# Block two's expert results are added to the tokens' sums one by one instead of through a sorted buffer

## What is computed

```python
hdn = silu(xc @ w1[e]) * (xc @ w3[e])            # 256 wide
ffn = sum over the token's two experts of weight * (hdn @ w2[e])
x = layernorm(DEEPNORM_ALPHA * x + g2 * ffn, ln2_g, ln2_b)
```

## Time and profile before

| | |
|---|---|
| Time, median of 3 runs | 989.95 us (989.67 to 990.65) |
| The profiled execution's own time | 991.67 us |
| Its span | 989.1 us |
| PE busy | 913.5 us (92%) |
| DVE busy | 547.4 us (55%) |
| ACT busy | 346.2 us (35%) |
| Read from HBM | 287.34 MB |
| Mean granted TensorE clock | 0.982 of full speed |

### The profile page before, as it was taken

The page is one execution under the profiler, slowest core; times in us unless marked ns, Lnnn a source line. Parts: engine busy times, 40 slices in busy tenths (PEclk is TensorE's granted clock), DMA queues, the critical chain, the costliest instruction groups (busy, mean ns, idle before and its releaser), DMA issues. The chain is left out here.

```text
span 989.1 us, 14610 instructions
## 1 busy us (share of the span) xinstructions
PE 913.5 (92%) x5308; PEld 552.8 (56%) x5308; DVE 547.4 (55%) x1106; ACT 346.2 (35%) x663; POOL 21.0 (2%) x41
## 2 busy tenths in 40 slices
PE   8999999999999998877787799999899999999995
PEld 6778656977967633322222389867643434343434
DVE  5736427555445747433333475887856655555556
ACT  5644434446345232221221356743531111111113
POOL 1000110000000000000000000000000000000000
PEclk9999999999999999998999899999999999999998
DMA  9355394455415999999999957530749999999931
GB/s 356 139 209 201 117 433 174 146 208 187 173 74 192 383 420 428 425 424 426 428 424 428 426 176 316 212 128 12 287 151 409 424 427 427 425 429 426 422 152 42
DMA packets 28894, 289.04 MB, mean 292 GB/s; under 512 B 3080, under 2 KB 5544, under 8 KB 7728
## 3 DMA queue, kind: packets, MB, share of 16 engines
q1 hardware_dynamic: 25344, 282.04, 69.0%
q0 software_dynamic: 1136, 3.74, 1.2%
q10 hardware_dynamic: 2368, 2.64, 0.9%
HBM read 287.34 MB, written 1.06 MB: 292 GB/s over the span
## 5 line engine op out<-in xcount | busy, mean ns | idle before, releaser
L1070 PE MATMUL bank<-ring,arena 128*64 128x512 f32 (+1 forms) x1024 | 188.9, 634 | 35.4 <-DMA ring<-in_experts 34.6
L508 DVE TENSOR_TENSOR ring_r<-ring,ring_r 128x1024 fp32r<-128x1024 f32 (+1 forms) x84 | 99.2, 1211 | 83.3 <-ACT ring_r L501 83.3
L1070 PEld LDWEIGHTS bank<-ring,arena 128*64 128x64 f32 (+1 forms) x1024 | 49.7, 126 | 131.0 <-issue 109.6
L501 ACT ACTIVATE ring_r<-ring 128x1024 fp32r<-128x1024 f32 (+1 forms) x84 | 84.8, 1046 | 74.4 <-PE bank L677 72.9
L675 PE MATMUL bank<-HT_r,ring_r 128*128 128x256 f32 x352 | 101.9, 289 | 2.6 <-DVE ring_r L508 1.8
L677 PE MATMUL bank<-HT_r,ring_r 128*128 128x256 f32 x352 | 99.6, 283 | 0.0
L1085 PE MATMUL bank<-ring,arena 128*64 128x512 f32 (+1 forms) x512 | 97.5, 609 | 0.3 <-DVE arena L2454 0.2
L1733 ACT ACTIVATE arena<-bank 128x512 f32<-128x512 f32 x64 | 38.2, 597 | 128.9 <-PE bank L1070 128.9
L676 PE MATMUL bank<-XN_r,ring_r 128*128 128x256 f32 x288 | 81.5, 283 | 0.0
L1727 ACT ACTIVATE arena<-arena 128x64 f32<-128x64 f32 (+1 forms) x64 | 18.1, 283 | 174.7 <-DVE arena L2444 174.7
L2419 DVE SCALAR_TENSOR_TENSOR arena_r<-bank,arena,arena_r 128x512 fp32r<-128x512 f32 x32 | 24.0, 750 | 97.6 <-ACT arena_r L1739 97.6
(11 more groups left out here) (472 smaller groups left out, 1457.1 us busy)
## 6 DMA issues: line engine op xcount, KB each, us to landing
ring<-in_experts SPq DMA_DIRECT2D x63, 2048.0 KB, 16.2
ring<-in_experts SPq DMA_DIRECT2D x63, 1024.0 KB, 13.5
ring<-in_ada SPq DMA_DIRECT2D x12, 2048.0 KB, 10.9
ring<-in_win SPq DMA_DIRECT2D x5, 2048.0 KB, 12.3
ring<-in_hy SPq DMA_DIRECT2D x3, 2048.0 KB, 19.8
ring<-in_mk SPq DMA_DIRECT2D x2, 2048.0 KB, 11.2
ring<-in_mv SPq DMA_DIRECT2D x2, 2048.0 KB, 12.0
ring<-in_wo SPq DMA_DIRECT2D x2, 2048.0 KB, 7.4
```

Source lines behind the costliest of these rows:

```text
L501: nc.scalar.activation(R(h), w, ACT.Copy).then_inc(sem("w_high"), 1)
L508: nc.vector.tensor_tensor(R(w), w, R(h), ALU.subtract).then_inc(sem("w_low"), 1)
L1070: last = mm(gu_bank[g:g + wide, :], xw[:, k, :], w[:, k * 512:(k + 1) * 512], start=k < sides, stop=k >= KD - sides)
```

## The change

Block two's experts work as block one's do. The four sums live in banks 0 to 3 from the router on: `start_sum` comes in two pairs, ahead of the gate's row and behind the counts, in place of some of the matmuls without a use. The gather has only banks 4 to 7, each used twice. VectorE makes the lists in place of `selw`. In a step, `down` adds both halves of the hidden part in one bank (128 rows: 64 slots for each half of the channels), VectorE multiplies by weight and gate in one instruction to `y_gated`, ScalarE rounds that to `y_high`, VectorE subtracts to `y_low`, and `to_tokens` takes the place of `down_T`. The gate's row is kept as `g2half`, 512 columns with another half of the channels in each half of the rows. The last expert's `down` moves behind the extras; `swT`, `ysT`, `pairs_T` and `scatter` are gone, and the three matmuls without a use inside an extra pass too.

```diff
-EXPERT = (4, 5, 6, 7)
-SUMS = (1, 2, 3, 4)
+EXPERT = {1: (6, 7, 5, 0), 2: (4, 5, 6, 7)}
...
-        + [(f"cnt{b}", 1)] + [("g2r", 2, (0, 1))] * (b == 2) + [(f"gx{b}", 8, ((3, 4, 5, 6, 7, 0, 1, 2), (4, 5, 6, 7, 0, 1, 2, 3))[b - 1])] \
-        + ([("bias", 1, (5,)), ("slots1", 1, (0,)), ("sct1", 4, SUMS)] if one else
-           [("swT2", 2, (6, 7)), ("yTa2", 4, EXPERT), ("sct2", 4, (0, 1, 2, 3)), ("yTb2", 4, EXPERT)])
+        + ([("cnt1", 1)] if one else [("sct2", 4, (0, 1, 2, 3)), ("cnt2", 1, (6,)), ("g2r", 2, (7, 4))]) \
+        + [(f"gx{b}", 8, ((3, 4, 5, 6, 7, 0, 1, 2), (4, 5, 6, 7, 4, 5, 6, 7))[b - 1])] \
+        + ([("bias", 1, (5,)), ("slots1", 1, (0,)), ("sct1", 4, (1, 2, 3, 4))] if one else [("slots2", 1, (5,))])
...
-                occupy(f"cnt{b}", 0, 6 if b == 2 else 8)
                 if b == 2:
-                    gate_row("g2r", diag2, "diag2")
+                    pe.wait_ge(sem("diag2"), 1)
+                    start_sum((0, 1))
+                    occupy("cnt2", 0, 2)
+                    pe.wait_ge(sem("diag2"), 2)
+                    gate_row("g2r", diag2)
...
-                occupy(f"gx{b}", 0, 6)
+                if b == 2:
+                    start_sum((2, 3))
+                occupy(f"gx{b}", 0, 6 if b == 1 else 1)
...
+                pe.wait_ge(sem("lists"), b)
+                ps = take(pe, f"slots{b}")
+                full(slot_lists(b, ps), f"slots{b}")
...
+                    ready(pe, "gx2", 4)
+                    for _ in range(3):
+                        mm(bank[EXPERT[2][0]][:, 0:256], ident, T("iota")[:, 0:256], start=True, stop=True)
...
                 def down(w, hb=hb):
-                    for half in range(2):
-                        for f in range(2):
+                    for f in range(2):
+                        for half in range(2):
                             o = f * D + half * 512
-                            g = wide * (f if b == 2 else 2 * half + f)
-                            last = mm(d_bank[half if b == 2 else 0][g:g + wide, :], hb[:, f, :], w[:, o:o + 512],
-                                      start=True, stop=True)
+                            g = 64 * half + 32 * f * (b == 1)
+                            last = mm(d_bank[g:g + wide, :], hb[:, f, :], w[:, o:o + 512],
+                                      start=b == 1 or f == 0, stop=b == 1 or f == 1)
...
-                    if 0 not in first and b == 1:
-                        pe.wait_ge(sem("y_low1"), e - 1)
-                        to_tokens(r % 2).then_inc(sem("to_tokens1"), 1)
-                    elif 0 not in first:
-                        pe.wait_ge(sem(f"d_lo{b}"), e - 1)
-                        pe.wait_ge(sem(f"d_hi{b}"), e - 1)
-                        if 2 not in first:
-                            pe.wait_ge(sem(f"y_out{b}"), e - 2)
-                        down_T().then_inc(sem(f"yT_done{b}"), 1)
+                    if 0 not in first:
+                        pe.wait_ge(sem(f"y_low{b}"), e - 1)
+                        to_tokens(r % 2).then_inc(sem(f"to_tokens{b}"), 1)
...
                 def weigh(e, i):
-                    act.wait_ge(sem("cur1"), e + 1)
-                    act.wait_ge(sem("down_done1"), e + 1)
-                    A_(R(y_high), d_bank[0][:, :], ACT.Copy, scale=cur[:, i, 1:2]).then_inc(sem("y_high1"), 1)
+                    if b == 1:
+                        act.wait_ge(sem("cur1"), e + 1)
+                        act.wait_ge(sem("down_done1"), e + 1)
+                    else:
+                        act.wait_ge(sem("y_gated2"), e + 1)
+                    high_part(i).then_inc(sem(f"y_high{b}"), 1)
...
+                def gated(i):
+                    return V.scalar_tensor_tensor(out=y_gated, in0=d_bank[:, :], scalar=cur[:, i, 1:2], in1=g2half,
+                                                  op0=ALU.mult, op1=ALU.mult)
...
                 def low_part(e, i):
+                    if b == 2:
+                        dve.wait_ge(sem("down_done2"), e + 1)
+                        gated(i).then_inc(sem("y_gated2"), 1)
+                    dve.wait_ge(sem(f"y_high{b}"), e + 1)
+                    y_rest(i).then_inc(sem(f"y_low{b}"), 1)
```

The extra pass of block two is now block one's. On VectorE it begins with three numbers read from the table and six instructions, and TensorE's `gate_up` waits for the last of them:

```diff
+                        s = dve.value_load(tabi[0:1, bass.ds(XSTART + j, 1)], min_val=0, max_val=NPAIR)
+                        rank = dve.value_load(tabi[0:1, bass.ds(XRANK + j, 1)], min_val=0, max_val=S - wide)
+                        ex = dve.value_load(tabi[0:1, bass.ds(XEXPERT + j, 1)], min_val=0, max_val=NE - 1)
+                        V.tensor_copy(xwin[:, 0], xsT[:, :, bass.ds(s, wide)])
+                        V.tensor_copy(turn_x[:, 0:wide], iota[:, bass.ds(rank, wide)]).then_inc(sem(f"cur{b}"), 1)
+                        dve.wait_ge(sem(f"cur{b}"), j * 3 + (NE + 1))
+                        rank_of_slot(b, turn_x[:, 0:wide]).then_inc(sem(f"extra_x{b}"), 1)
```

More of the change, by code:

```diff
@@ L445, in expert_banks @@
         def expert_banks(b):
-            if b == 1:
-                return bank[6], bank[7], [bank[5], bank[0]], None
-            base = place("yTa2", 0)[0]
-            at = [bank[(base + i) % 8] for i in range(6)]
-            return at[4], at[5], at[0:2], at[2:4]
+            return [bank[i] for i in EXPERT[b]]
         def slot(i):
@@ L1144, in step @@
                     if 1 not in first:
+                        if isinstance(e, int) and e == 1:
+                            ready(pe, f"slots{b}")
                         pe.wait_ge(sem(f"gu_sb{b}"), e)
@@ L1216, in moe @@
-                pe.wait_ge(sem("d_lo2"), NE)
-                pe.wait_ge(sem("y_out2"), NE - 1)
-                down_T(range(4))
-                pe.wait_ge(sem("d_hi2"), NE)
-                down_T(range(4, KD)).then_inc(sem("yT_done2"), 1)
+                pe.wait_ge(sem(f"y_low{b}"), NE - 1)
+                to_tokens(0).then_inc(sem(f"to_tokens{b}"), 1)
+                pe.wait_ge(sem("routed"), b)
+                n = pe.value_load(tabi[0:1, XCOUNT:XCOUNT + 1], min_val=0, max_val=NX[b] - 1)
@@ L1223, in moe @@
                         w = ring[:, slot(base), :]
-                        pe.wait_ge(sem("extra_x2"), j + 1)
-                        pe.wait_ge(sem("extra_w2"), j * 16 + 16)
-                        gate_up(xwin[:, 0], w).then_inc(sem("extra_gu2"), 1)
-                        pe.wait_ge(sem("extra_gs2"), j + 1)
-                        gu_T().then_inc(sem("extra_gT2"), 1)
-                        for _ in range(3):
-                            mm(d_bank[0][:, 0:256], ident, T("iota")[:, 0:256], start=True, stop=True)
@@ L1242, in pairs_T @@
-                def pairs_T(stage, js):
-                    for j in js:
-                        pt, half = j // 2, j % 2
-                        ps = take(pe, stage, j % 4)
-                        for c in range(4):
-                            last = tr(ps[:, c * P:(c + 1) * P], ysT[:, 4 * half + c, pt * P:(pt + 1) * P], ident)
-                        full(last, stage, j % 4)
-                def scatter(pt):
-                    stage = (f"yTa{b}", f"yTb{b}")[pt // 2]
-                    end = pt == NPAIR // P - 1
-                    for q in range(4):
-                        t, half = (q // 2, q % 2) if end else (q % 2, q // 2)
-                        ready(pe, stage, 2 * (pt % 2) + half)
-                        tok, cols = slice(t * P, (t + 1) * P), slice(half * 512, (half + 1) * 512)
-                        mm(acc[2 * t + half][:, :], R(swT[:, pt, tok]), R(ytok[:, pt, cols]), start=False, stop=False)
-                        last = mm(acc[2 * t + half][:, :], R(swT[:, pt, tok]), R(ytok_low[:, pt, cols]),
-                                  start=False, stop=end)
-                        if end:
-                            full(last, f"sct{b}", 2 * t + half)
@@ L1265, in moe @@
-                pairs_T(f"yTa{b}", range(0, 4))
-                scatter(0)
-                pairs_T(f"yTb{b}", range(4, 6))
-                scatter(1)
-                pairs_T(f"yTb{b}", range(6, 8))
-                scatter(2)
-                scatter(3)
+                        pe.wait_ge(sem(f"extra_x{b}"), j + 1)
+                        pe.wait_ge(sem(f"extra_w{b}"), j * 16 + 16)
+                        gate_up(xwin[:, 0], w).then_inc(sem(f"extra_gu{b}"), 1)
+                        slot_lists(b, list_bank)
@@ L1273, in _ @@
+                pe.wait_ge(sem(f"y_low{b}"), NE)
+                to_tokens(1, True)
             moe(1)
@@ L1697, in moe @@
                 if b == 2:
-                    copies("g2r", [g2row[:, 0:512], g2row[:, 512:1024]])
+                    for j in range(2):
+                        ps = got(act, "g2r", j)
+                        rows = slice(64 * j, 64 * j + 64)
+                        free(A_(g2half[rows, :], ps[rows, :], ACT.Copy), "g2r", j)
                 for k in range(0, KD, 2):
@@ L2609, in moe @@
[L2609 to L2619 removed]
+                            dve.wait_ge(sem("extra_down2"), j + 2)
```

364 lines of the change are left out of this document (101 added, 263 removed).

## The result

| | before | with the change |
|---|---|---|
| Time, median | 989.95 us (988.92 to 991.73, 9 runs) | 993.47 us (991.48 to 995.17, 9 runs) |
| The profiled execution's own time | 991.67 us | 991.48 us |
| Its span | 989.1 us | 988.9 us |
| PE busy | 913.5 us | 901.3 us |
| DVE busy | 547.4 us | 517.6 us |

The ratio after to before is 1.0027, 95% interval 1.0016 to 1.0038: 2.7 us slower (1.6 to 3.7); the two medians of the table lie 3.5 us apart. The forecast was 991.3 us, within a range of 987.6 to 995.2. The measured median lies 2.2 us above the forecast and inside the range. Measured a second time beside other runs of the kernel before, the ratio was 1.0015 (1.0004 to 1.0026). The prediction counts less than 0.2% as no change: the first measurement lies just beyond that, the second within it.

The account below looks back on a forecast made before the run. TensorE was taken as the bound (busy 92%, alone in the chain of block two's experts). Router +0.6, step +2.6, end -4.7 and clock +3.0 make +1.5 us: about 991.3 us, rounded down from the 989.95 median; range 987.6 to 995.2.

Parts of the forecast that it names:

- the router's term: Block two's router: VectorE starts earlier but the four-bank gather stalls, first `gate_up` 0.6 us later; bounds 0 and +1.5.
- the step: Block two's expert loop: `to_tokens` for `down_T` lengthens each of 29 steps by 0.09 us, +2.6 us; bounds 0 and +6.
- the end: Last `gate_up` to the last layer norm's first read: 31.9 us instead of 36.6, so -4.7 us.
- the clock: Tail: TensorE's waits bring two low stretches (half clock, 1.2 GHz), +3.0 us; bounds 0 and +10.
- within 0.2%: Whole kernel: time changes by less than 0.2% (2 us), counted as no change; chance 0.44.
- slower: Whole kernel: slower by more than 0.2%; chance 0.36.
- the forecast's own 989.5 to 993: Whole kernel: the time range of the forecast itself, without the rivals; chance 0.45.
- the rival with three or four low stretches: Tail: clock stays low for three or four stretches, +3.6 to +5.3 us, 993.5 to 995.3 us; chance 0.18.
- the first rival: Tail: the clock holds or falls once, sum -1.5 to 0, 988.4 to 990 us; chance 0.22.
- The rival of adds side by side: Loop: adds run in pairs, step shrinks by 0.24 us until weights bound it, -6.5 us, 983.5 us; chance 0.10.
- The slack of the weights: Last expert: gate and up weights land 5.4 us before TensorE wants them, so shorter steps gain at most that.

Follow-up runs that it names:

- Experiment 2: Kernel before, with one of `down_T`'s eight transposes done twice in every step: 995.19 us, ratio 1.0032.
- experiment 1: Changed kernel, with matmuls without a use ahead of each of TensorE's five waits in block two's tail: 990.55 us, ratio 0.9990.
- experiment 3: Changed kernel, with block two's `to_tokens` adding only the high part except for the last expert: 989.40 us, ratio 0.9978.
- e9: Changed kernel, with the three dropped matmuls without a use put back in block two's extra pass: 993.85 us, ratio 1.0029.
- experiment 6: Changed kernel, last expert's `down` ahead of the extra pass, window copied earlier, separate buffers; three runs: 983.71, 984.20 (with matmuls without a use), 982.52 us (repeat).
- experiment 4: Changed kernel, its extra pass copying the window and releasing `gate_up` before the two other table reads and the ranks: 992.85 us, ratio 1.0009.
- e7: Changed kernel, last expert's `down` ahead of the extra pass, window copied earlier, plus matmuls without a use in TensorE's waits: 984.20 us, ratio 0.9926.
- e6: Changed kernel, last expert's `down` ahead of the extra pass, window copied earlier, no matmuls without a use: 983.71 us, ratio 0.9919.

## Why the prediction came out as it did

The forecast had four terms, three of them with the right sign, and its sum, +1.5 us, was lower than the +2.7 of the first measurement and equal to the second's. Part of that is luck: by the profiles the router's term was 0.8 us too high, and the step, the end and the clock 0.6, 0.5 and 0.7 too low. The forecast gave "within 0.2%" a chance of 0.44 and "slower" 0.36, so what the first measurement shows was not its likeliest outcome. The median of 993.47 us also lies above the forecast's own 989.5 to 993, next to the rival with three or four low stretches; the traces show two. Step by step:

- **The step: right, a size off.** +0.09 us was predicted from block one's rows, and 0.11 was measured, so +2.6 became +3.2. `to_tokens` takes 0.12 us more than `down_T` up to `down`'s start, and `down` keeps the 1.87 us that it takes behind `down_T`. For that case the prediction's upper bound had 0.2 us a step, which was too much. There is no idle time ahead of `to_tokens` or `down`. Experiment 2 makes the same loss by another means and finds it whole at the end.
- **The router: wrong sign, small.** +0.6 was predicted and -0.2 measured. The gather stalled for 0.51 us and not 1.4. (By its own numbers the prediction's stall was 1.3: 720.6 and 0.74 make 721.3.) The step that failed is the start of VectorE's reading: I kept the 0.67 us of idle time ahead of it that the trace of before shows, behind two table reads. In the changed kernel these reads happen earlier, the first at 715.9 us, while VectorE still works off instructions that it already has, and the reading starts at 717.60 with no idle time. Before, both stood behind a wait of VectorE (at 720.9 and 721.5). That the missing wait is the cause is read from these times; no run tested it.
- **The end: right within 0.5 us once the clock is taken out.** 31.9 us was predicted without the clock, and experiment 1 shows 32.4. (Two sums in that count are 0.1 us off, 25.3 and not 25.4 behind the first hops, which moves nothing.) The extra pass's `gate_up` starts 14.7 us behind the last one and not 13.85: the reads and the branch leave VectorE idle for 2.09 us, where I took 1.2 (the bounds 0.7 and 2.5 held it). All later distances were met within 0.2 us: `gate_up` to `down` 7.12 (predicted 7.1), to `to_tokens` 4.18 (4.35), to the last `down` 1.12 (1.1), to the layer norm 5.31 (5.45). Against the 36.7 us of before the end gives -4.2, where -4.7 was predicted.
- **The clock: right, and somewhat larger.** Two low stretches were predicted for +3.0 (1.7 and 1.3), and two were found: on the extra pass's `gate_up`, as named, +1.94, and on a later group, the last `down`, +1.52. Two further groups lost 0.1 and 0.3 us. Together it is +3.7, as the tails of the changed kernel and of experiment 1 tell (36.1 and 32.4). This term decides the result: with the clock held the change comes out at 0.9990, which can't be told from no change, as the first rival said. By the Trainium skill ("TensorE: Matmul & The Clock Gate", section "Part 1: The HAM clock gate (the "warmup" mystery)") the low level is the default and activity lifts it; the tails agree with that, 0.99 with the waits filled (experiment 1) and 0.81 with waits of 1.65 to 4.60 us. All four profiles with a wait of 4.5 to 5.1 us ahead of the extra pass's `gate_up` (the change and its repeat, experiment 3 and e9) have it slow, 5.41 to 6.28 us.
- **The rival of adds side by side: the mechanism is there, the gain isn't.** A matmul of the gather, 512 columns with 128 rows, takes 0.235 us (7.52 by 32); the eight adds with 64 rows take 1.14 to `down`'s start, 0.142 each, and in experiment 3 four of them take 0.67, so that the other four cost 0.47, 0.118 each, half a gather's. I read this as adds that run in pairs already, and did in block one's rows that I had priced them by; no run put the halves in another order to test it. By the Trainium skill ("TensorE: Matmul & The Clock Gate", section "Part 3: Packing small matmuls — row/col tiling") matmuls in different row groups run at the same time, and the estimate of 0.86 us that I made from it (0.85 by its own terms) comes near the 0.94 (8 by 0.118) that the adds cost at the margin; the rest of the 1.14, 0.20, is what such a group costs beyond them. The rival's error was to count as a further gain what the row already contained.
- **The slack of the weights: wrong.** I gave it as 5.4 us, by adding the median landing time (15.7 us) to the last request. But the landing times grow along the loop; for the requests between 760 and 775 us the median is 13.1. This is the view of DMA issues in the trace of before again, for the request of 920.75 alone:

```profile
ring<-in_experts SPq DMA_DIRECT2D x1, 2048.0 KB, 20.0
```

It landed at 940.75, 1.0 us ahead of the `gate_up` that wants it (941.76). Experiment 3 shows the same: it took 0.47 us from each step, and the loop became 1.0 us shorter than before. The weights come at 427 GB/s in the kernel before too (850 to 900 us), 7.37 us an expert, and the old step of 7.07 was already shorter than that: it lived on the lead with which the loop begins. The forecast didn't rest on it, since its steps grew, but the rival's time did.

With the measured sizes the sum is -0.2 +3.2 -4.2 +3.7 = +2.5 us. Where did the time go that the removed turns back (`pairs_T`, `scatter`) gave? TensorE was busy for 10.6 us less in the tail (32.60 to 22.03), the slower groups included, and the tail became 0.6 us shorter. The work that is gone was replaced by waits: one for the table reads, two for round trips through three engines, and the clock that fell in them. Experiment 6 shows that this was the order of the work: with the window read and the last `down` ahead of the pass the same arithmetic beats the kernel before by 8 us.

## What to carry to other kernels

When a change takes work from an engine at the end of a program, write down what it then waits for: if that is a chain through other engines, look for work that can stand in it (here the last expert's `down`) before counting the saved time. Matmuls without a use can buy back the clock in such a chain, but real work in the same place buys back the wait too: here the tail became 11 us shorter (some 9 without the earlier table read, by the estimate in experiment 6) against 4. For a weight stream's slack, divide bytes by the measured rate over the whole loop, or read the landing time of the request in question, rather than adding the loop's median to it.

## What the runs showed of the hardware that was not expected

- A number read from a table into a register costs VectorE 0.65 us of idle time alone and 2.09 us for three with a branch, when VectorE has nothing queued; in the changed kernel's router, behind queued work, two cost nothing (no idle time at 717.20 or 717.60). The trace lists each read with 0.30 us, and three of them 0.75 us apart (953.3, 954.1, 954.8):

```profile
L2416 DVEq TENSOR_LOAD <-tabi x1: 303/303/303, 953.3 to 953.3; - x1
L2417 DVEq TENSOR_LOAD <-tabi x1: 303/303/303, 954.1 to 954.1; - x1
L2418 DVEq TENSOR_LOAD <-tabi x1: 303/303/303, 954.8 to 954.8; - x1
```

- The granted clock fell behind waits of 2.2 us as well (experiment 4), whereas the waits of 0.3 to 1 us that experiment 1 left didn't cost it in that run's profile. In the repeat of experiment 6 it fell in a tail that had kept it in the first run: with the same program it isn't the same each time.
- Matmuls without a use are not free where they delay what stands behind them: e7's tail is 2.1 us longer than e6's in the profiles, although their medians (984.20 and 983.71) can't be told apart. Against e6's repeat, whose clock fell, it is 0.4 us longer.
